# One cross-attention key tile moved into the first post-norm seam of a two-block transformer kernel, with the memory norm beside the output projection

## The reference, cut to what matters

```python
# first block
hn  = rms_norm(x, norm_mix_pre)
mix = hybrid_mixer(hn, ...)              # ends in y @ w_out
x   = x + rms_norm(mix, norm_mix_post)   # "the first seam": post0
hn  = rms_norm(x, norm_ffn_pre)
x   = x + rms_norm(conv_ffn(hn, ...), norm_ffn_post)   # ff0, post1
# second block, layer 0
x = x + pool_conv_mixer(rmsnorm(x, norm_mix_g[0]), ...)   # pc_in, conv, pool, pc_out
m = rmsnorm(mem, norm_mem_g[0])          # mem is 256 x 1024
k, v = split(m @ wkv)                    # k is 8 tiles "mem_k0", v is "mem_v0"
x = x + cross_attention(rmsnorm(x, norm_xa_g[0]), k, v)
...
```

## Time and profile before

| | before |
|---|---|
| median of the runs shown | 1999.33 us (1999.08 to 2000.58) |
| the profiled execution | 1998.99 us, of which span 1997.2 us |
| PE busy | 1983.2 us (99% of the span) |
| POOL busy | 1447.2 us (72%) |
| DVE busy | 973.9 us (49%) |
| ACT busy | 614.0 us (31%) |
| granted TensorE clock, mean | 0.998 |

### The profile page before, as it was taken

One profiled execution on the slowest core, in us unless ns is written; L12 is line 12 of the kernel. 1 busy time (PEld: TensorE's weight loads), 2 busy tenths in 40 slices (PEclk: granted clock), 3 DMA queues, 4 the chain that ended last, 5 costly groups with the idle time before them and its releaser, 6 DMA issues.

```text
span 1997.2 us, 25808 instructions
## 1 busy us (share of the span) xinstructions
PE 1983.2 (99%) x9499; PEld 1631.3 (82%) x9499; DVE 973.9 (49%) x1612; ACT 614.0 (31%) x1176; POOL 1447.2 (72%) x736
## 2 busy tenths in 40 slices
PE   9999999999999999999999999999999999999998
PEld 7788778888888888888888888877678888888887
DVE  5566445243443899565431422464656553223134
ACT  6554442221014345433210110226743331011012
POOL 7633379777877877964977778687569398777774
PEclk9999999999999999999999999999999999999999
DMA  5742233232223345321322223224013123233322
GB/s 177 136 65 64 85 110 109 99 99 95 95 85 116 106 147 167 108 81 47 116 95 95 95 95 106 74 96 128 1 38 111 43 95 106 95 96 99 101 82 66
DMA packets 58683, 190.99 MB, mean 96 GB/s; under 512 B 6416, under 2 KB 10256, under 8 KB 58576
## 3 DMA queue, kind: packets, MB, share of 16 engines
q1 hardware_dynamic: 54720, 184.42, 29.9%
q10 hardware_dynamic: 3856, 5.07, 0.9%
HBM read 183.50 MB, written 2.10 MB: 93 GB/s over the span
## 4 chain that ended last, share of the span: by engine, by line
PE 92%; DVE 6%; ACT 1%; DMA 0%; issue 0%; POOL 0%; SPq 0%; DVEq 0%; POOLq 0%
PE bank L755 28%; PE bank L757 28%; PE bank L756 28%; DVE bank L2887 3%; PE bank L1523 2%; PE bank L1190 1%; PE bank L1537 1%; PE bank L1553 1%; PE bank L1101 1%; DVE memL L2355 0%; PE bank L1045 0%; PE bank L1273 0%; PE bank L1212 0%; DMA raw<-weights 0%; DVE bank L2865 0%
## 5 line engine op out<-in xcount | busy, mean ns | idle before, releaser
L642 POOL TENSOR_TENSOR wH<-raw,zero 128x1024 fp32r<-128x1024 f32 (+1 forms) x303 | 578.7, 1910 | 372.1 <-PE bank L757 352.1
L645 POOL TENSOR_TENSOR wL<-raw,wH 128x1024 fp32r<-128x1024 f32 (+1 forms) x303 | 719.3, 2374 | 23.8
L755 PE MATMUL bank<-hnH,wH 128*128 128x512 f32 x1443 | 565.0, 392 | 3.9 <-DVE hnL L2544 3.0
L756 PE MATMUL bank<-hnL,wH 128*128 128x512 f32 x1443 | 562.2, 390 | 0.0
L757 PE MATMUL bank<-hnH,wL 128*128 128x512 f32 x1443 | 562.1, 390 | 0.0
L755 PEld LDWEIGHTS bank<-hnH,wH 128*128 128x128 f32 x1443 | 271.7, 188 | 62.9 <-DVE hnL L2544 3.4
L757 PEld LDWEIGHTS bank<-hnH,wL 128*128 128x128 f32 x1443 | 271.5, 188 | 56.3
L756 PEld LDWEIGHTS bank<-hnL,wH 128*128 128x128 f32 x1443 | 271.7, 188 | 55.3
L755 PE MATMUL bank<-actH,wH 128*128 128x512 f32 (+1 forms) x802 | 309.7, 386 | 0.0
L757 PE MATMUL bank<-actH,wL 128*128 128x512 f32 (+1 forms) x802 | 308.6, 385 | 0.0
L756 PE MATMUL bank<-actL,wH 128*128 128x512 f32 (+1 forms) x770 | 296.0, 384 | 0.0
(11 more groups left out here) (451 smaller groups left out, 2616.9 us busy)
## 6 DMA issues: line engine op xcount, KB each, us to landing
raw<-weights SPq DMA_DIRECT2D x315, 512.0 KB, 3.4
raw<-weights SPq DMA_DIRECT2D x28, 384.0 KB, 2.9
XT<-x_t SPq DMA_DIRECT2D x8, 256.0 KB, 6.5
XT<-x_t ACTq DMA_DIRECT2D x1, 2048.0 KB, 9.3
maxB<-rowM SPq DMA_DIRECT2D x7, 256.0 KB, 17.2
out<-MIX SPq DMA_DIRECT2D x13, 128.0 KB, 1.9
qkO<-qkA SPq DMA_DIRECT2D x4, 256.0 KB, 4.4
memT<-mem_t ACTq DMA_DIRECT2D x1, 1024.0 KB, 5.4
```

The source lines that it names most:

```text
L642: nc.gpsimd.tensor_tensor(wH[:, slot, 0:w], raw[:, slot, 0:w], nothing.broadcast_to([P, w]), ALU.add)\
L645: nc.gpsimd.tensor_tensor(wL[:, slot, 0:w], raw[:, slot, 0:w], wH[:, slot, 0:w].bitcast(F32), ALU.subtract).then_inc(split, 1)
L755: mm(out_, aH, bH, start=first, stop=False)
L756: mm(out_, aH, bL, start=False, stop=False)
```

## The change

- The first key tile of `mem_k0` becomes a weight unit between `w_out` and `ff0_gu0`. POOL makes both its halves, and PE runs it between the sums of the first seam and the first matmuls of ff0. Its result waits in `keys0` and is copied to its place in the second seam. Around `post1` there are still four key tiles, each one later in number, and the conv stage has three where it had four.
- The memory's transfer is issued before `w_out`. ACT squares it into `KT[1]`, DVE adds in a PSUM bank, PE sums behind result 3 of `w_out`, ACT takes the root in PSUM, and DVE scales `memT` ahead of its work on result 4 and makes all eight low halves `memL` ahead of its work on result 5.
- PE's sum of `ssq` moves from behind the last unit of `w_out` to ahead of that unit's chunk 6. ACT's copy of the last result moves behind the first root.
- In ff0's first three units, chunks 1 to 7 go by halves: for each chunk the six matmuls on `hnH`, then the three on `hnL`. Low half 1 goes from POOL to DVE.
- In the conv stage the places of the pool groups and of `conv_mean` are shifted.

The diff, cut to its core:

```diff
...
+    elif _n == "w_out":
+        SEQ += [("w_out", _i) for _i in range(_c)] + [("mem_k0", _i) for _i in range(EARLY)]
...
-MEMORY += [POS["mem_k0", _i] for _i in range(8)]
+MEMORY += [POS["mem_k0", _i] for _i in range(EARLY, 8)]
...
-TILES += [("w_out", (0, 1, 2)), ("norm_b", (2, 3)), ("w_out", range(3, 8)), ("post0", 2)]
+TILES += [("w_out", (0, 1, 2)), ("norm_b", (2, 3)), ("w_out", (3,)), ("mem_sums", 1),
+          ("w_out", range(4, 8)), ("mem_k0s", 1), ("post0", 2)]
...
-                    for c_ in range(1, KD, 2):
+                    for c_ in range(3, KD, 2):
...
+                def by_halves(k, tiles):
+                    high_ready(k)
+                    for i in tiles:
+                        slot = POS[name, i] % RING
+                        for w in (wH, wL):
+                            mm(psum(TILE0[name] + i)[:, :], w[:, slot, k * P:k * P + P], bH[:, k, :], start=False, stop=False)
+                    ready(k)
+                    for i in tiles:
+                        last = mm(psum(TILE0[name] + i)[:, :], wH[:, POS[name, i] % RING, k * P:k * P + P], bL[:, k, :],
+                                  start=False, stop=k == kd - 1)
+                        if k == kd - 1:
+                            last.then_inc(unit_done, 1)
...
+                                high_ready=(lambda k: pe.wait_ge(hi_ready, KD * NORM[norm] + k + 1)) if f == 0 else None,
...
-                            after={3: lambda: row_sums(TILE0["mem_sums"], "mem", MEM)} if (f, t) == (0, 0) else {},
...
-            project("w_out", actH, actL, ready=mixed_ready, lead=3)
+            def square_sums():
+
+                gone_wait(pe, TILE0["w_out"] + KD - 2)
+                for s_ in range(2):
+                    n = TILE0["post0"] + s_
+                    claim(n)
+                    mm(psum(n)[:, ENDS[s_]], ones, ssq[:, ENDS[s_]], start=True, stop=False)
+
+            def memory_sums():
+
+                n = TILE0["mem_sums"]
+                pe.wait_ge(sig("mem_sum"), 1)
+                claim(n)
+                mm(psum(n)[:, 0:MEM], ones, lnb[:, 0:MEM], start=True, stop=True).then_inc(tile_done, 1)
+            project("w_out", actH, actL, ready=mixed_ready, lead=3, after={3: memory_sums},
+                    within={(KD - 1, 6): square_sums})
...
-                gone_wait(pe, TILE0["w_out"] + KD - 2)
-                for s_ in range(2):
-                    claim(n + s_)
-                    mm(psum(n + s_)[:, ENDS[s_]], ones, ssq[:, ENDS[s_]], start=True, stop=False)
...
+            for i in range(EARLY):
+                memory_key(i)
             feed_forward(0, "ffn_pre")
-            memory_key(0)
+            memory_key(EARLY)
             post_sums("post1")
-            for i in (1, 2, 3):
+            for i in range(EARLY + 1, EARLY + 4):
...
-            for i in range(4, 8):
+            for i in range(EARLY + 4, 8):
                 memory_key(i)
             memory_values(0, 0)
-            memory_values(0, 1, after={2: lambda: pool_group(0)})
+            memory_values(0, 1, after={3: lambda: pool_group(0)})
             project("mem_k1", memH[1], memL[1], cols=MEM, ready=lambda k: wait_hn("mem1", k), lead=2,
-                    after={1: lambda: pool_group(1), 5: lambda: pool_group(2)})
-            memory_values(1, 0, after={1: lambda: pool_group(3)})
-            memory_values(1, 1, after={1: conv_mean})
+                    after={2: lambda: pool_group(1), 6: lambda: pool_group(2)})
+            memory_values(1, 0, after={2: lambda: pool_group(3)})
+            memory_values(1, 1, within={(2, 1): conv_mean})
...
+            act.dma_start(memT[:, :, :], mem_t.rearrange("(k p) m -> p k m", p=P)).then_inc(mem_in, 16)
...
+                        if s_ == 0:
+                            free(run(MIX[:, KD - 1, :], psum(TILE0["w_out"] + KD - 1)[:, :], ACT.Copy), TILE0["w_out"] + KD - 1)
...
-                    if first == 0 and c_ % 2:
+                    if first == 0 and c_ % 2 and c_ > 1:
...
+                if first == 0:
+                    n = key_tile(0)
+                    tile_wait(act, n)
+                    free(run(keys0[:, :, :], psum(n)[:, 0:EARLY * MEM].rearrange("p (t m) -> p t m", t=EARLY), ACT.Copy), n)
...
+            act.wait_ge(mem_in, 48)
+            for c_ in range(KD):
+                run(KT[1][:, c_, :], memT[:, c_, :], ACT.Square).then_inc(sig("mem_sq"), 1)
             for m in range(KD):
+                if m == 4:
+                    n = TILE0["mem_sums"]
+                    tile_wait(act, n)
+                    link(run(psum(n)[:, 0:MEM], psum(n)[:, 0:MEM], ACT.Ln, bias=v("eps"), scale=1.0 / D))
+                    run(psum(n)[:, 0:MEM], psum(n)[:, 0:MEM], ACT.Exp, scale=-0.5).then_inc(sig("mem_root"), 1)
+                elif m == 5:
+                    memory_input(0)
...
+            run(KT[0][:, 0:EARLY, :], keys0[:, :, :], ACT.Copy)
+            for i in (EARLY, EARLY + 2):
...
-                dve.wait_ge(mem_in, 48)
-                for c_ in range(KD):
-                    add_squares(c_ == 0, MEM)
+                n = TILE0["mem_sums"]
+                root = psum(n)[:, 0:MEM]
                 dve.wait_ge(sig("mem_root"), 1)
                 for c_ in range(KD):
-                    tt(memT[:, c_, :], memT[:, c_, :], rmem[:, :], ALU.mult).then_inc(sig("mem_normed"), 1)
+                    ins = tt(memT[:, c_, :], memT[:, c_, :], root, ALU.mult)
...
-                            if m == 0:
-                                memory_norm()
...
-                            memory_low(0, m)
...
+                    if (first, c_) == (0, 2):
+                        new_low(1)
...
+            acc = psum(TILE0["norm_b"] + 3)[:, 0:MEM]
+            gone_wait(dve, TILE0["norm_b"] + 3)
+            for c_ in range(KD):
+                dve.wait_ge(sig("mem_sq"), c_ + 1)
+                square_ = KT[1][:, c_, :]
+                if c_ == 0:
+                    link(nc.vector.tensor_copy(acc, square_))
+                elif c_ < KD - 1:
+                    link(tt(acc, acc, square_, ALU.add))
+                else:
+                    tt(lnb[:, 0:MEM], acc, square_, ALU.add).then_inc(sig("mem_sum"), 1)
             for m in range(KD):
+                if m == 4:
+                    memory_norm()
+                elif m == 5:
+                    for c_ in range(KD):
+                        memory_low(0, c_)
...
```

More of the change, by code:

```diff
@@ L406, in program @@
         rkv = at("rkv", [P, S], offset=up2 + 5632)
+        keys0 = at("keys0", [P, EARLY, MEM], offset=up2 + 5632)
         assert up2 + 5632 + 2048 <= TOP, (up2, TOP)
@@ L707, in _ @@
                 if kind == "memory":
+                    rest = n % RING
+                    for j in range(rest):
+                        slot = (u0 + j) % RING
+                        pool.wait_ge(sig("memory_hi"), taken[0] + j + 1)
+                        nc.gpsimd.tensor_tensor(wL[:, slot, 0:w], raw[:, slot, 0:w], wH[:, slot, 0:w].bitcast(F32),
+                                                ALU.subtract).then_inc(split, 1)
                     with pool.Fori(0, n // RING) as i:
-                        for j in range(RING):
+                        for j in range(rest, rest + RING):
                             slot = (u0 + j) % RING
@@ L760, in wait_hn, with project @@
                 pe.wait_ge(hn_ready, KD * NORM[norm] + k + 1)
-            def project(name, bH, bL, kd=KD, cols=S, ready=None, after={}, lead=0, order=None, late=0, ends=None):
+            def project(name, bH, bL, kd=KD, cols=S, ready=None, after={}, lead=0, order=None, late=0, ends=None,
+                        high_ready=None, within={}):
                 order = range(COUNT[name]) if order is None else order
+                def by_halves(k, tiles):
[10 more added lines that the diff above has]
+                            last.then_inc(unit_done, 1)
                 def part(i, k):
@@ L799, in project, with project_natural @@
                         after[at_]()
-            def project_natural(name, aH, aL, kd, blocks, tile0, u0, units, after={}):
+            def project_natural(name, aH, aL, kd, blocks, tile0, u0, units, after={}, within={}):
                 for i in range(units):
@@ L1991, in memory_key @@
                 tile_wait(act, n)
-                if l == 0 and i < 4:
-                    free(run(KT[0][:, 2 * (i // 2):2 * (i // 2) + 2, :],
+                if l == 0 and i < EARLY + 4:
+                    free(run(KT[0][:, i:i + 2, :],
                              psum(n)[:, :].rearrange("p (t m) -> p t m", t=2), ACT.Copy), n)
@@ L2045, in conv_statistics @@
                         cvb[:, c_, :] if c_ < 2 else psum(TILE0["conv"] + c_)[:, :], ACT.Square).then_inc(sig("ln_sq"), 1)
-            for i in range(28):
+            for i in range(EARLY, 28):
                 if i == 27:
@@ L2548, in new_low @@
                     dve.wait_ge(sig("x_copied_back"), first + c_ + 1)
-                    if post == "post0" and c_ % 2:
```

(5 more changed lines are left out.)

76 lines of the change are left out of this document (41 added, 35 removed).

## The result

The changed kernel takes 2010.08 us (median of 5 runs, 2009.75 to 2011.86), the kernel before 2000.16 us beside it: a ratio of 1.0052, 95% interval 1.0041 to 1.0064. That is slower by about 10 us, and outside my range, whose upper end was 2006.0. The profiled execution took 2009.75 us with a span of 2008.0, 10.8 more than before.

The account below looks back on a forecast made before the run. PE, busy for 1983.2 us, was taken to bound the kernel. Parts 0.1 - 2.66 + 6.7 = +4.1 us on 1998.99, plus 0.34 for the median, gave 2003.4 us; own range 2001.8 to 2005.2, over all 1996.7 to 2006.0.

Parts of the forecast that it names:

- The first `w_out` results and POOL's start at 241.21 stay.: Early in w_out: a stated sign of the forecast, that nothing moves there; no us were priced for it.
- Part 3, the wait: In w_out: eight low halves wait for POOL operations, so PE waits 5.5 us for result 6's sum; Part 3 totals +6.7.
- Part 3, the clock: Behind the new w_out hole: granted clock falls as behind the 3.04 us hole, costing 1.25 us.
- The rival of a deeper hole: In w_out: DVE starts one POOL operation later (2.4 us), or the clock stays at 0.50 longer; 2005.8 us, chance 0.09.
- Part 2, the conv stage: Work leaving ff0 (-0.43) and the conv stage (-2.88), less 0.65 of new waits: -2.66 us.
- Part 1, the seam: From w_out to ff0's fifth chunk, if nothing new waits: 1.53 later, 1.45 regained, +0.1 us.
- +0.87 and -0.27: Seam terms for moving the sum of ssq: last result 0.87 us later, addition of the last squares 0.27 sooner.
- No new hole: In w_out: low halves follow each other or fall into POOL's pauses, done by 268.5; -2.6 us, 1996.8 us, chance 0.15.
- The key tile does not hide: At the seam: POOL's ring runs late, PE pays up to 2.88 us again; 2006.3 us with the hole, chance 0.04.

Follow-up runs that it names:

- e1: Changed kernel with the issues of posI and pwt back behind the first post-norm on ACT's queue, memT's staying early: 2005.5 us, ratio 1.0028.
- e3: Kernel before with only the issues of memT, posI and pwt moved directly behind XT's on ACT's queue: 2003.57 us, ratio 1.0019.
- e8: Changed kernel with the eight low halves reading the root's PSUM bank in place of memT (memL then not correct): 2003.69 us, ratio 1.0016.
- e6: Changed kernel with posI/pwt issues back, low halves spread, memory norm one result sooner, ACT's VM copies ahead of its tap wait: 1996.73 us, ratio 0.9986.
- e9: As e6, but each chunk of the seam's leading tiles waits for its low half before its high-half matmuls, as before: 1997.91 us, ratio 0.9992.
- e10: As e6, but with the two sums of ssq back behind the last w_out tile: 1996.18 us, ratio 0.9983.
- e2: Changed kernel with the eight low halves as a tensor_scalar reading memT alone (memL then not correct): 2010.68 us, ratio 1.0050.
- e4: Changed kernel with posI's and pwt's issues as in e1 and DVE's eight low halves spread over results 5 to 7: 2000.81 us, ratio 1.0005.
- e12: As e6, but the moved key tile is made in the conv stage again, with that stage's places of before: 1999.68 us, ratio 0.9998.
- e11: Changed kernel with ACT's four issues in the order XT, posI, pwt, memT: 2004.67 us, ratio 1.0027.

## Why the prediction was wrong, step by step

The mechanism that decided the sign was right, and the size was missed by 6.7 us of 10.8. In the profiled runs I had +4.1, and +10.8 came.

- **The failed step: "The first `w_out` results and POOL's start at 241.21 stay."** I listed the memory's transfer as part of the change and then gave none of the three moved issues a price, though ACT stands in front of PE there. They stood directly ahead of ACT's head roots, and one held the queue for 4.01 us. It is worth 4.3 us in the traces (4.57 from `w_out`'s first matmul), 4.6 by e1 and 3.8 by e3. Without it the time is e1's 2005.5 us, still above the forecast's own 2001.8 to 2005.2, and inside the range over all. The trace of before could not show a 4 us issue, but it shows ACT's squares directly ahead of a sum of PE there, so a stall of ACT beyond its small slack (its squares came 4.4 us later and PE waited 2.72) could land on PE, and a clock dip with it. I should have priced that as a rival.
- **Part 3, the wait.** Predicted 5.5, measured 5.24. Eight low halves at about 2.2 us (2.12), the sum ready about 5.5 behind PE's question, all confirmed; e8 shows the cause by taking it away. The scalings ran free, as I used it. DVE reached the low halves at 259.92, which is 255.6 plus the 4.3 from above.
- **Part 3, the clock.** Predicted 1.25, measured 2.3 (e8), and 1.7 to 2.7 over five executions. I had copied the loss behind the 3.04 us hole to one of 5.24 us. The stretches show 1.2 GHz from 278 to beyond 282 instead of 2.75 us. The rival of a deeper hole named this ("the clock stays at 0.50 longer") but had a price only for one more POOL operation, which did not come.
- **Part 2, the conv stage.** I took 0.65 of new waits and named `conv_mean` and the gates as places. The wait came elsewhere, 1.85 us at the value tiles, behind ACT's copies of the taps. Of 0.43 + 2.88 I expected 2.66 back, and 1.6 came (12.4 less 10.8): a term mis-sized by 1.05.
- **Part 1, the seam.** Predicted +0.1. In e6, where nothing new waits, from the first copy of `w_out` to the fifth chunk takes 284.94 - 240.44 = 44.50 us, before 285.20 - 241.06 = 44.14: +0.36. From ff0's start to the fifth chunk I said 9.4, it took 297.56 - 288.10 = 9.46, and e9 gives back 10.83. The key tile is hidden and the clock stays at 1.00 in e6, as stated. The terms for the moved sum, +0.87 and -0.27, are borne out too: e10 takes the move back and gains 0.8.
- **The rivals.** "No new hole" was priced at 1996.8 us. Its condition didn't hold in the changed kernel. e6 makes it hold and takes 1996.7. That the two agree so closely is in part luck: 1996.8 stood on the 1999.33 of before and a gain of 2.6, and e6 gains 3.2 on the 1999.93 beside it and 2.2 in the traces from `w_out`'s first matmul on, with edits that the priced kernel did not have. "The key tile does not hide" is out.

Added up: 4.3 (issues) + 1.05 (clock) + 1.05 (conv stage) = 6.4 us of a miss of 6.7. The seam (+0.26) and the wait (-0.26) cancel, and some 0.3 us are not assigned. What stays open: what the queue runs out of behind 3 MB, and why the same 1.86 us wait draws the clock down in one execution and not in another.

## What to carry to other kernels

Every instruction that an edit moves needs a price where it lands, DMA issues first: on an engine that others wait for, put small issues ahead of large ones. Beside a GpSimd that never paused, each VectorE operation of the tried forms with all its tensors in SBUF cost about one GpSimd operation here (2.02 to 2.12 us against 0.40), so spread such operations where nobody waits, or keep one input in PSUM. When a hole in PE's work is priced, add the slow matmuls behind it; and check, where work is taken out of a stage, which engine does not come sooner with it. And compare two traces from the last instruction ahead of the edit, not from the start of the span: in e10 that turns the result around.

## What the runs showed of the hardware that I had not expected

- A 2 KB issue on ACT's queue took 3.90 to 4.26 us (after, e2, e3, e8) behind 2 MB and 1 MB issued in the 1.1 us before, 0.60 behind the 2 MB alone, 0.34 ahead of both. The engine stands still meanwhile (ACT idle for 4.57 us).
- A VectorE `tensor_scalar` from SBUF to SBUF waits for GpSimd like an operation with two SBUF inputs: 2.02 against 2.12 us, and 0.40 with one input in PSUM.
- A wait of about 1.86 us of PE left the granted clock at 1.00 in six executions and brought it to 0.50 in two (e2, e8), worth 1.6 us. It was also 0.50 in a stretch behind the hole of 2.09 us in e4, and behind those of 3.04, 3.53 and 5.24 us (before, e12, after).
- The price of the low clock did not follow the hole: 1.7 us behind 5.25 us (e11), 2.3 behind 5.24 (after), 2.7 behind 4.48 (e2).
